# Moving a GpSimd burst, a pair of small products and the level masks of a triangular inverse in a hybrid RG-LRU / RWKV-7 decoder step

## The reference

```
P = xn @ w_in                         # (tokens, 14784)
w = -softplus(-(w0 + tanh(wd) @ w2)) - 0.5 ; decay = exp(-exp(w))
a = sigmoid(a0 + ad @ a2)             # low-rank products
kk = normalize(k * k_kk) ; k = k * (1 + (a - 1) * k_a) ; b = kk * a
step: sa = S @ (-kk_t)
      S  = S * w_t + sa b_t^T + v_t k_t^T
      y  = S @ r_t
```

## Time and profile before

| | us |
|---|---|
| median of 3 runs | 2690.89 (2689.9 to 2691.99) |
| the profiled execution, its own time | 2693.02 |
| its span | 2691.0 |
| busy TensorE, VectorE, ScalarE, GpSimd | 2573.5, 1604.7, 1129.1, 86.3 |
| mean granted TensorE clock | 0.983 of full |

### The profile page before, as it was taken

One profiled execution on the slowest core, in us unless ns is written; L12 is line 12 of the kernel. 1 busy time (PEld: TensorE's weight loads), 2 busy tenths in 40 slices (PEclk: granted clock), 3 DMA queues, 4 the chain that ended last, 5 costly groups with the idle time before them and its releaser, 6 DMA issues.

```text
span 2691.0 us, 58316 instructions
## 1 busy us (share of the span) xinstructions
PE 2573.5 (96%) x23356; PEld 2413.5 (90%) x23356; DVE 1604.7 (60%) x2770; ACT 1129.1 (42%) x1514; POOL 86.3 (3%) x59
## 2 busy tenths in 40 slices
PE   5999999999999999999899999999999999999997
PEld 4988888888888888888799999999999999999996
DVE  5667777676667767676344556654444444445665
ACT  3544555554444455544243333444323333423333
POOL 0000000000000000000000000000000000000000
PEclk8999999999999999999999999999999999999998
DMA  5643333334343343334366766555655665656653
GB/s 155 153 109 91 97 98 92 94 93 108 94 109 89 86 107 94 94 92 111 91 174 188 217 187 166 163 165 168 168 163 160 168 168 159 172 160 167 168 141 97
DMA packets 699658, 361.60 MB, mean 134 GB/s; under 512 B 43905, under 2 KB 698531, under 8 KB 698659
## 3 DMA queue, kind: packets, MB, share of 16 engines
q1 hardware_dynamic: 699598, 360.76, 49.7%
HBM read 346.13 MB, written 14.59 MB: 134 GB/s over the span
## 4 chain that ended last, share of the span: by engine, by line
PE 83%; DVE 10%; issue 3%; ACT 2%; DMA 2%; DVEq 0%; SPq 0%; ACTq 0%
PE bank L615 82%; DVE wl L1681 2%; DVE sd L1669 1%; DVE both L1346 1%; PE bank L644 1%; DVE yc L1349 1%; DVE ysq L1346 1%; DMA raw<-w_in 1%; DMA gb_scratch<-gat 1%; DVE inv L1346 0%; ACT L1093 0%; DVE nrm L1349 0%; DVE sd L1352 0%; DVE ar L1349 0%; DVE bv L1349 0%
## 5 line engine op out<-in xcount | busy, mean ns | idle before, releaser
L615 PE MATMUL bank<-xh,wh 128*128 128x288 f32 (+1 forms) x3136 | 1004.4, 320 | 16.1 <-DVE xl L1346 8.8
L615 PE MATMUL bank<-xh,wl 128*128 128x288 f32 (+1 forms) x3136 | 933.3, 298 | 1.1 <-issue 1.1
L615 PE MATMUL bank<-xl,wh 128*128 128x288 f32 (+1 forms) x3136 | 933.8, 298 | 0.0
L615 PEld LDWEIGHTS bank<-xh,wh 128*128 128x128 f32 x3136 | 594.6, 190 | 55.9 <-issue 14.8
L1343 DVE TENSOR_TENSOR wl<-raw,wh 128x2048 fp32r<-128x2048 f32 x206 | 472.0, 2291 | 233.6 <-ACT wh L1037 233.6
L615 PEld LDWEIGHTS bank<-xl,wh 128*128 128x128 f32 x3136 | 595.9, 190 | 7.3
L615 PEld LDWEIGHTS bank<-xh,wl 128*128 128x128 f32 x3136 | 595.7, 190 | 0.0
L615 PE MATMUL bank<-sbh,wl 128*128 128x288 f32 x1792 | 534.0, 298 | 0.0
L615 PE MATMUL bank<-sbh,wh 128*128 128x288 f32 x1792 | 529.6, 296 | 1.7 <-DVE wl L1343 1.7
L615 PE MATMUL bank<-sbl,wh 128*128 128x288 f32 x1792 | 529.5, 295 | 0.0
L1037 ACT ACTIVATE wh<-raw 128x2048 fp32r<-128x2048 f32 x206 | 392.6, 1906 | 285.7 <-PE bank L615 276.3
(11 more groups left out here) (276 smaller groups left out, 2435.2 us busy)
## 6 DMA issues: line engine op xcount, KB each, us to landing
raw<-w_in SPq DMA_DIRECT2D x116, 1024.0 KB, 5.8
raw<-w_up SPq DMA_DIRECT2D x64, 1024.0 KB, 6.2
raw<-w_down SPq DMA_DIRECT2D x64, 1024.0 KB, 5.8
raw<-w_rg_o SPq DMA_DIRECT2D x16, 1024.0 KB, 6.0
raw<-w_rw_o SPq DMA_DIRECT2D x16, 1024.0 KB, 5.9
raw<-w_o SPq DMA_DIRECT2D x16, 1024.0 KB, 5.9
raw<-w_ple_gate SPq DMA_DIRECT2D x16, 1024.0 KB, 6.0
s<-state_rwkv SPq DMA_DIRECT2D x32, 128.0 KB, 4.0
```

Of the source, the lines that this page charges most:

```text
L615: return pe.matmul(out, lhsT, rhs, start=start, stop=stop, skip_group_check=True)
```

## The change

1. GpSimd's `samples` waits for `pair_read` instead of `ar_ready`; `pair_read` is now given by VectorE once per step, when both factors of the inverse are made.
2. `wd` and `ad` become one stage `lowrank` in slot 8: both products go out back to back, to `bank[7]` and `bank[3]` (which waits for `ab_read` of the chain before), and both sigmoids follow each other on ScalarE. `kp` and `ksq` get slot 10. `state_in` gets a wait for `siga`, since it reuses `bank[3]`.
3. In `pairwise` VectorE first makes `tt` straight from PSUM (two products of 128 columns and the addition of the identity) and releases TensorE's first product with it, then `tn` (`pair_read`), and then the rest of `ams` (two products of 384 columns).
4. `am` and `level_masks` are gone. TensorE multiplies the unmasked `ab` with `tt` into `bank[6]`, and VectorE multiplies the result by the level's mask as it reads it from PSUM into `yy`; ScalarE's copy is gone.

```diff
-    9: ["wd"],
-    10: ["ad"],
+    8: ["lowrank"],
+    10: ["kp", "ksq"],
...
 # TensorE
-                if name == "wd":
+                if name == "lowrank":
...
+                        pe.wait_ge(ab_read, 2 * it)
                     mm(bank[7][:, 0:NT], w2s[0:RW, :], low[0:RW, 0, :], True, True).then_inc(low_mm, 1)
-                elif name == "ad":
-                    pe.wait_ge(sig_ready, 2 * it + 1)
-                    mm(bank[7][:, 0:NT], a2s[0:RA, :], low[0:RA, 1, :], True, True).then_inc(low_mm, 1)
+                    mm(bank[3][:, 0:NT], a2s[0:RA, :], low[0:RA, 1, :], True, True).then_inc(low_mm, 1)
...
-                        if l == 2:
-                            pe.wait_ge(am_ready, count)
+                        if l == 1:
+                            pe.wait_ge(ab_read, 2 * one)
                         for q, out, rc in halves:
-                            done = mm(out[rc, q * CHUNK:(q + 1) * CHUNK], am[rc, l - 1, q, :], tt[rc, q, :], True, True)
+                            done = mm(out[rc, q * CHUNK:(q + 1) * CHUNK], ab[rc, q, :], tt[rc, q, :], True, True)
                         done.then_inc(yy_mm, 1)
                     else:
                         pe.wait_ge(yy_read[l - 1], count)
+                        if l == 1:
+                            pe.wait_ge(pair_read, count)
...
                     pe.wait_ge(ab_read, 2 * one)
+                    if not last:
+                        pe.wait_ge(sig_ready, 2 * one + 2)
 # ScalarE
-                elif name[:6] == "invert" and name[7] == "a":
-                    act.wait_ge(yy_mm, 5 * p + int(name[6]))
-                    act.activation(yy[:].rearrange("p a b -> p (a b)"), bank[5][:, 0:256], ACT.Copy).then_inc(yy_read[int(name[6]) - 1], 1)
 # VectorE, pairwise
+                    for h in range(2):
+                        dve.wait_ge(pair_mm, 3 * p + h + 1)
+                        tt_(tt[:, 2 * h:2 * h + 2, :], pairs[h][:, :, 0:CHUNK], first, ALU.mult).then_inc(ch.sem, ch.one())
+                    dve.wait_ge(ch.sem, ch.so_far())
+                    tt_(tt, tt, eye, ALU.add).then_inc(tn_ready[0], 1)
                     dve.wait_ge(ab_read, 2 * one)
                     tt_(tn, ab[:], cst[:, C_LM:C_LM + CHUNK].unsqueeze(1).to_broadcast([P, 4, CHUNK]), ALU.mult).then_inc(ch.sem, ch.one())
                     dve.wait_ge(ch.sem, ch.so_far())
+                    tt_(tn, tn, eye, ALU.add).then_inc(pair_read, 1)
+                    masks = cst[:, C_AM + CHUNK:C_AM + 256].unsqueeze(1).to_broadcast([P, 2, 192])
+                    for h in range(2):
+                        tt_(ams[:, 2 * h:2 * h + 2, CHUNK:256], pairs[h][:, :, CHUNK:256], masks, ALU.mult).then_inc(ch.sem, ch.one())
+                elif name[:6] == "invert" and name[7] == "a":
+                    l = int(name[6])
+                    half_mask = cst[:, C_LM + l * CHUNK:C_LM + (l + 1) * CHUNK].unsqueeze(1).to_broadcast([P, 4, CHUNK])
+                    dve.wait_ge(yy_mm, 5 * p + l)
+                    tt_(yy[:], bank[6][:, 0:256].rearrange("p (q t) -> p q t", q=4), half_mask, ALU.mult).then_inc(yy_read[l - 1], 1)
 # GpSimd
-                pool.wait_ge(ar_ready, p + 1)
+                pool.wait_ge(pair_read, p + 1)
```

More of the change, by code:

```diff
@@ L80, in constants @@
     for l in range(6):
-        c[:, C_LM + l * CHUNK:C_LM + (l + 1) * CHUNK] = half(i, j, 2 ** l)
+        c[:, C_LM + l * CHUNK:C_LM + (l + 1) * CHUNK] = half(j, i, 2 ** l) if l else half(i, j, 1)
     row, t = np.arange(P)[:, None], np.arange(SAMP)[None, :]
@@ L106 @@
 U_PLE = U_FFN + 8 * KT
-STEPS = {"dve_rg": 40, "dve_ch": 32}
+STEPS = {"dve_rg": 40, "dve_ch": 35}
 ROW_LOADS = 27
@@ L221, in program @@
             sbk, vpad = skv[:, 0, :], skv[:, 1, :]
-            both = mb("both", [P, 9 * 4 * CHUNK])
+            both = mb("both", [P, 32 * CHUNK])
             ams = both[:, 0:16 * CHUNK].rearrange("p (q t) -> p q t", q=4)
-            am = both[:, 16 * CHUNK:].rearrange("p (l q t) -> p l q t", l=5, q=4)
             ab, yy = mb("ab", [P, 4, CHUNK]), mb("yy", [P, 4, CHUNK])
@@ L294, in program @@
         gout_mm, gout_read, bt_ready, bonus_mm, bonus_read = sems("gout_mm gout_read bt_ready bonus_mm bonus_read")
-        pair_mm, pair_read, ab_read, am_ready, yy_mm, tn_mm = sems("pair_mm pair_read ab_read am_ready yy_mm tn_mm")
+        pair_mm, pair_read, ab_read, yy_mm, tn_mm = sems("pair_mm pair_read ab_read yy_mm tn_mm")
         yy_read = sems("yy_read1 yy_read2 yy_read3 yy_read4 yy_read5")
@@ L766, in stage @@
                     l, part, count = int(name[6]), name[7], apart(one)
-                    halves = [(q, bank[5], slice(c * CHUNK, (c + 1) * CHUNK)) for q in range(4) for c in range(2)]
+                    halves = [(q, bank[6], slice(c * CHUNK, (c + 1) * CHUNK)) for q in range(4) for c in range(2)]
                     if part == "a":
                         pe.wait_ge(tn_ready[l - 1], count)
-                        if l == 2:
-                            pe.wait_ge(am_ready, count)
+                        if l == 1:
+                            pe.wait_ge(ab_read, 2 * one)
                         for q, out, rc in halves:
-                            done = mm(out[rc, q * CHUNK:(q + 1) * CHUNK], am[rc, l - 1, q, :], tt[rc, q, :], True, True)
+                            done = mm(out[rc, q * CHUNK:(q + 1) * CHUNK], ab[rc, q, :], tt[rc, q, :], True, True)
                         done.then_inc(yy_mm, 1)
@@ L1088, in early @@
                 one = it + 1
-                if name == "wd":
+                if name == "lowrank":
+                    act.wait_ge(low_mm, 2 * it + 1)
+                    act.activation(sigw[:], bank[7][:, 0:NT], ACT.Sigmoid, bias=ptu[:, W0:W0 + 1]).then_inc(sig_ready, 1)
+                    act.wait_ge(low_mm, 2 * it + 2)
+                    act.activation(siga[:], bank[3][:, 0:NT], ACT.Sigmoid, bias=ptu[:, A0:A0 + 1]).then_inc(sig_ready, 1)
+                elif name == "ksq":
                     act.wait_ge(mixed, 3 * it + 1)
                     act.activation(ksq[:], zk[:], ACT.Square, scale=ptu[:, KK:KK + 1]).then_inc(ksq_ready, 1)
[L1092 to L1096, removed]
                 elif name == "decay":
@@ L1499, in early @@
                 one = it + 1
-                if name == "ad":
+                if name == "kp":
                     dve.wait_ge(sig_ready, 2 * it + 2)
@@ L1546, in early @@
                     dve.tensor_copy(vv[:, :, SAMP:], zv[:, samp_all].unsqueeze(1).to_broadcast([P, 2, SAMP])).then_inc(early_end, 1)
[L1548 to L1553, removed]
             def stage(name, p, ch):
@@ L1607, in stage @@
                 elif name == "pairwise":
-                    masks = cst[:, C_AM:C_AM + 256].unsqueeze(1).to_broadcast([P, 2, 256])
+                    pairs = [bank[4 + h][:].rearrange("p (g t) -> p g t", g=2) for h in range(2)]
+                    eye = cst[:, C_ID2:C_ID2 + HEAD].unsqueeze(1).to_broadcast([P, 4, CHUNK])
+                    first = cst[:, C_AM:C_AM + CHUNK].unsqueeze(1).to_broadcast([P, 2, CHUNK])
                     for h in range(2):
                         dve.wait_ge(pair_mm, 3 * p + h + 1)
-                        tt_(ams[:, 2 * h:2 * h + 2, :], bank[4 + h][:].rearrange("p (g t) -> p g t", g=2), masks, ALU.mult).then_inc(pair_read, 1)
+                        tt_(tt[:, 2 * h:2 * h + 2, :], pairs[h][:, :, 0:CHUNK], first, ALU.mult).then_inc(ch.sem, ch.one())
@@ L1612, in stage @@
+                    dve.wait_ge(ch.sem, ch.so_far())
+                    tt_(tt, tt, eye, ALU.add).then_inc(tn_ready[0], 1)
                     dve.wait_ge(ab_read, 2 * one)
                     tt_(tn, ab[:], cst[:, C_LM:C_LM + CHUNK].unsqueeze(1).to_broadcast([P, 4, CHUNK]), ALU.mult).then_inc(ch.sem, ch.one())
-                    eye = cst[:, C_ID2:C_ID2 + HEAD].unsqueeze(1).to_broadcast([P, 4, CHUNK])
-                    dve.wait_ge(pair_read, 2 * one)
-                    tt_(tt, ams[:, :, 0:CHUNK], eye, ALU.add).then_inc(ch.sem, ch.one())
@@ L1617, in stage @@
-                    if later:
-                        dve.wait_ge(yy_mm, 5 * p)
-                    level_masks(0, 1)
-                    dve.wait_ge(ch.sem, ch.so_far())
-                    tt_(tn, tn, eye, ALU.add).then_inc(tn_ready[0], 1)
-                    level_masks(1, 5).then_inc(am_ready, 1)
+                    dve.wait_ge(ch.sem, ch.so_far())
+                    tt_(tn, tn, eye, ALU.add).then_inc(pair_read, 1)
+                    masks = cst[:, C_AM + CHUNK:C_AM + 256].unsqueeze(1).to_broadcast([P, 2, 192])
@@ L1626, in stage @@
                     dve.wait_ge(tn_ready[l - 1], one)
+                    if l == 1:
+                        dve.wait_ge(pair_read, one)
                     n = 512 if l < 5 else 256
-                    tt_(inv[:, 0:n], inv[:, 0:n], bank[5][:, 0:n], ALU.add).then_inc(tn_ready[l], 1)
+                    tt_(inv[:, 0:n], inv[:, 0:n], bank[6][:, 0:n], ALU.add).then_inc(tn_ready[l], 1)
```

## The result

The changed kernel takes 2709.5 us (median of 4 runs, 2707.2 to 2712.6) against 2691.4 before: ratio 1.0068, interval 1.005 to 1.0085. It is 18 us slower. Of the kernels further down, one run of "masks 2 and 4 ahead" was a slow one (2766.6 us at a mean granted clock of 0.85, where its other three have 0.991); it counts in the 2644.5 but not in the ratio. The profiled execution took 2708.7, with a span of 2706.5.

A forecast was written before the change was run, and what follows sets the result against it. TensorE, busy 96% of the span, was taken as the bound. Steady steps +10, first step +4.3, step 0 -0.4, last step -11 and clock falls +13.6 gave +16 on the median: 2707 us, range 2678 to 2721.

The forecast's parts named there:

- The old waits go: TensorE's waits before the first product (2.11 us) and for `sigw` (1.21) vanish, 3.3 us per steady step.
- GpSimd under the token mix: GpSimd holds VectorE's `zk` mix, so level one's mask is late: new TensorE wait of 1.0 us, bounds 0 to 2.1.
- The mask at level two: Second mask stands behind 7.28 us of VectorE work: new TensorE wait of 2.0 us, bounds 1.8 to 2.3.
- order and not load: Masks on VectorE: what is queued ahead of each 0.42 us mask decides; 7.28 us ahead at level two.
- Level four: Mask ends at 918.99 behind VectorE's queue, wanted at 917.75: new TensorE wait of 1.3 us, bounds 1.1 to 1.5.
- levels three and five: Masks ready in time, no TensorE wait: estimated 0.9 us to spare at three, 0.3 at five.
- Per steady step: Gone 3.3 us, new waits 4.3: 1.0 us slower against a step without a fall of the clock.
- The old falls: Clock falls in 8 of 14 steady steps of the kernel before, 0.5 us net each, taken off the +14.
- The last step: Waits for ScalarE's `yy` copies and `inv` and two clock falls go, some 1.5 us returns at level two: -11 us.
- The clock: After the level-two wait, 8 new falls of TensorE's clock at 1.7 us each: +13.6 us.
- Rivals 1 and 2: Clock stays up: idle time split in three, 2694, chance 0.15; or GpSimd misses the mix, 2679, chance 0.2.
- Rival 3: Clock falls in each of the 15 steps: +28.5 us, 2719, chance 0.2.

The follow-up runs named there:

- masks 2 and 4 ahead: Changed kernel with VectorE's masks of levels two and four moved ahead in its own queue: 2644.5 us, 0.9820 against before.
- Parts 1 to 3: Changed kernel without its fourth part, masked matrices and ScalarE's copies put back: 2641.4 us, 0.9816 against before.
- parts 2 and 3: Changed kernel without its fourth part and with GpSimd released by `ar_ready` again: 2659.7 us, 0.9876 against before.
- part 2 alone: Kernel before with only the low-rank part: both products in slot 8, sigmoids back to back: 2659.0 us, 0.9872 against before.
- mask 2 ahead: Changed kernel with only the mask of level two moved ahead in VectorE's queue: 2661.4 us, 0.9886 against before.
- part 4 alone: Kernel before with only VectorE applying level masks from PSUM, `am` and ScalarE's copies gone: 2729.5 us, 1.0136 against before.
- changed, GpSimd as before: Changed kernel with GpSimd released by `ar_ready` again instead of `pair_read`: 2722.4 us, 1.0116 against before.
- mask 4 ahead: Changed kernel with only the mask of level four moved ahead in VectorE's queue: 2687.9 us, 0.9981 against before.
- GpSimd later alone: Kernel before with only GpSimd's release moved, to the step's first `tn_ready`: 2731.3 us, 1.0143 against before.

## Why the prediction was right

The forecast was 2707 and slower; it came out at 2709.5, and by the waits that were named. By its own steps:

- **The old waits go.** Right: none at the first product, none for `sigw`, `wl` and the square at their plain durations.
- **GpSimd under the token mix, 1.0 us at level one.** Right in the mechanism, the term was over-sized: 0.43, and none in step 1. The fused operation was held (1.18). The Trainium skill ("SBUF — State Buffer", Who interferes with whom) says so of any VectorE instruction with two SBUF inputs beside a GpSimd instruction that reads SBUF; the trace agrees. But the mix came when GpSimd's first operation was nearly over, and the fused operation waited 0.66 for the third and not a whole 1.05: the mix was held for 1.6 us and began 0.29 late (that gap stands there without GpSimd too), 1.9 together, where I had added 2.4.
- **The mask at level two, 2.0 us.** Right: 2.24. The queue ahead of it was 7.28 us, as read; TensorE's own way was 0.1 us shorter than I took it and the hand-over 0.1 longer. The prediction's point that this is order and not load was tested by moving the mask, and holds.
- **Level four, 1.3 us.** Right: 1.31. None at levels three and five: right.
- **Per steady step +1.0.** 0.7 (75.9 to 76.6), for what level one had too much. The old falls, taken at 0.5 each in the same sum, had cost 0.2 (75.9 to 76.1).
- **The last step, -11.** Right: -12.2, with one wait of 1.68 at level two.
- **The clock, 8 falls of 1.7.** 11 falls of 1.4 (76.6 to 78.0), so 15 us against 13.6. The count was a little low and the size a little high.

Some of the closeness is luck: 9 us too much for level one (15 x 1.0 where 14 x 0.43 came) and 1 too little gained in the last step stand against 3 too little for level two, 2 for the clock, 2 for the old falls and 1 at the start of the kernel. That last one is no effect of the change: where the chain starts varies from 132.6 to 135.5 us over the twelve traces. And the traces differ by 15.5 us, where the medians differ by 18.0.

Rivals 1 and 2 supposed that the clock stays up. In steps 1 to 15 it did so in the six kernels whose longest waits in the chain there are at most 1.3 us, and in none of those with a wait of 1.6 or more. Rival 3, falls in every step, came near in their number, 11 of 15, though not in the time (2719).

The sum of the parts would have misled: alone on the kernel before, part 1 costs 39 us, part 4 costs 38, part 2 gains 33. Parts 1 to 3 together gain 50.

## What to carry to other kernels

Before an operation is moved to another engine, write down what stands ahead of it there between the event that releases it and the use that waits for it: 0.42 us of work was late by 2.2 us behind 7.3 us of others' work, and on time once placed ahead of the last 3.0 of them. When an engine waits for a chain of several others, price each part of a change in the company of the rest: a part that only uncovers the next wait can be a loss alone and a gain when that wait is gone too. GpSimd's move costs 39 us alone and is worth 18 beside parts 2 and 3.

## What the runs showed of the hardware

A fall of TensorE's clock is not a fixed price. In the kernel before it cost 0.2 us a step, as it ran inside a wait that was coming anyway; in the changed kernel 1.4; with a wait of 3.6 us it lasted 6.8 us instead of 3.4. Waits of 1.1 to 1.3 us lowered the clock in none of steps 1 to 15 in three kernels (part 2 alone, parts 2 and 3, mask 2 ahead). Those of 1.9 did in 10 of 14 steps (part 4 alone), and those of 2.1 to 2.2 in 8 of 14 (before), 10 of 14 (changed), 11 of 14 (changed, GpSimd as before) and 6 of 14 (mask 4 ahead). So neither every long wait brings a fall nor does its length alone say which will. GpSimd and VectorE give way to each other an operation at a time: with GpSimd later alone a difference of 32 columns took 1.27 us, and 0.18 where GpSimd does not run beside it (before). Products with one operand in PSUM (1.01 for 2 x 384 columns) and an operation with a single SBUF operand (0.14) ran beside GpSimd at their plain time.
